# The low half of h in a split-fp32 feed-forward stage: GpSimdE's subtraction replaced by a ScalarE negation and an adding DMA

## The reference

```
x += 0.5 * (silu(rms(x) @ w1) * (rms(x) @ w3)) @ w2        # first feed-forward, d_ff = 2816
x += concat(window attention, gated chunk mixing) @ w_out + b_out
x += 0.5 * (silu(rms(x) @ w1') * (rms(x) @ w3')) @ w2'     # second feed-forward
x += sigmoid(rms(x) @ w_ple_gate) * (p @ w_ple_proj)
y  = rms(x)
```

## Time and profile before

| | |
|---|---|
| median of 3 runs | 987.37 us (985.55 to 987.81) |
| the profiled execution's own time | 986.51 us |
| its span, first to last instruction | 984.8 us |
| mean granted TensorE clock | 0.997 |
| TensorE matmul busy | 963.6 us, 98% |
| VectorE busy | 672.4 us, 68% |
| ScalarE busy | 458.7 us, 47% |
| GpSimdE busy | 260.5 us, 26% |
| h_lo on GpSimdE (L1101) | 18 instructions, 46.9 us |

### The profile page before, as it was taken

The page is one execution under the profiler, slowest core; times in us unless marked ns, Lnnn a source line. Parts: engine busy times, 40 slices in busy tenths (PEclk is TensorE's granted clock), DMA queues, the critical chain, the costliest instruction groups (busy, mean ns, idle before and its releaser), DMA issues.

```text
span 984.8 us, 19296 instructions
## 1 busy us (share of the span) xinstructions
PE 963.6 (98%) x7949; PEld 947.1 (96%) x7949; DVE 672.4 (68%) x1063; ACT 458.7 (47%) x750; POOL 260.5 (26%) x150
## 2 busy tenths in 40 slices
PE   6999999999999999999999999999999999999997
PEld 4999999999999999999899999999999999999997
DVE  5899658856768654457775399857766758855576
ACT  6645425533435443566444455424543443545243
POOL 2302202211111226332318411301221211114521
PEclk9999999999999999999999999999999999999999
DMA  7962433252243336321114693253324325235202
GB/s 216 163 127 70 124 105 99 76 145 72 75 128 99 97 85 184 102 65 44 44 55 129 128 172 97 61 145 97 96 80 116 97 60 144 65 98 161 87 22 88
DMA packets 191603, 101.38 MB, mean 103 GB/s; under 512 B 12955, under 2 KB 189429, under 8 KB 191501
## 3 DMA queue, kind: packets, MB, share of 16 engines
q1 hardware_dynamic: 175904, 90.23, 32.2%
q0 software_dynamic: 11440, 5.77, 4.7%
q10 hardware_dynamic: 4172, 4.15, 1.4%
HBM read 97.59 MB, written 3.59 MB: 103 GB/s over the span
## 4 chain that ended last, share of the span: by engine, by line
PE 91%; DVE 5%; ACT 1%; DMA 1%; issue 1%; SPq 0%; DVEq 0%; ACTq 0%
PE ps L1723 49%; PE ps L1803 36%; PE ps L2141 2%; PE ps L1759 1%; DMA x_rows<-in_x_prompt_dram 1%; PE ps L2015 1%; PE ps L2044 1%; DVE w_lo L1327 0%; PE ps L1754 0%; DVE w_lo L1419 0%; PE ps L1748 0%; DVE xb_lo L1216 0%; DVE tt L1437 0%; DVE mix_lo L1550 0%; PE ps L2165 0%
## 5 line engine op out<-in xcount | busy, mean ns | idle before, releaser
L1803 PE MATMUL ps<-xo_hi,w_hi 128*128 128x260 f32 x1008 | 284.2, 282 | 0.7 <-DVE ab L1350 0.7
L1803 PE MATMUL ps<-xo_lo,w_hi 128*128 128x260 f32 x1008 | 284.7, 282 | 0.0
L1803 PE MATMUL ps<-xo_hi,w_lo 128*128 128x260 f32 x1008 | 284.4, 282 | 0.0
L1723 PE MATMUL ps<-h_hi,w_hi 128*128 128x260 f32 x960 | 195.8, 285 | 0.7 <-issue 0.6
L1723 PE MATMUL ps<-h_hi,w_lo 128*128 128x260 f32 x960 | 193.4, 283 | 0.0
L1723 PE MATMUL ps<-h_lo,w_hi 128*128 128x260 f32 x960 | 193.4, 283 | 0.0
L1803 PEld LDWEIGHTS ps<-xo_hi,w_hi 128*128 128x128 f32 x1008 | 189.6, 188 | 0.9 <-issue 0.9
L1803 PEld LDWEIGHTS ps<-xo_hi,w_lo 128*128 128x128 f32 x1008 | 189.8, 188 | 0.0
L1803 PEld LDWEIGHTS ps<-xo_lo,w_hi 128*128 128x128 f32 x1008 | 189.7, 188 | 0.0
L1723 PEld LDWEIGHTS ps<-h_hi,w_hi 128*128 128x128 f32 x960 | 148.1, 189 | 1.7 <-issue 1.2
L1723 PEld LDWEIGHTS ps<-h_lo,w_hi 128*128 128x128 f32 x960 | 148.8, 189 | 0.0
(11 more groups left out here) (276 smaller groups left out, 1476.5 us busy)
## 6 DMA issues: line engine op xcount, KB each, us to landing
w_raw<-in_w_ffn_dram SPq DMA_DIRECT2D x88, 256.0 KB, 3.0
w_a<-in_w_ffn_dram SPq DMA_DIRECT2D x36, 512.0 KB, 4.8
w_raw<-in_w_ffn_dram SPq DMA_DIRECT2D x48, 384.0 KB, 3.2
w_raw<-in_w_ffn_dram SPq DMA_DIRECT2D x16, 512.0 KB, 7.0
w_lo<-in_w_ffn_dram POOLq DMA_DIRECT2D x11, 512.0 KB, 8.4
w_raw<-in_w_in_dram SPq DMA_DIRECT2D x10, 512.0 KB, 4.0
w_raw<-in_w_ple_gate_dram SPq DMA_DIRECT2D x8, 512.0 KB, 3.6
x_rows<-in_x_prompt_dram SPq DMA_DIRECT2D x4, 512.0 KB, 5.7
```

Of the source, the lines that this page charges most:

```text
L1723: ins = pe.matmul(ps[:, bank + step * h, 0:HALF], w[:, c, w0:w0 + P], m_[:, sk, h * HALF:(h + 1) * HALF], start=(first and n == 0), stop=( ...
L1803: ins = pe.matmul(ps[:, b, 0:Q], w[:, c, k * P:(k + 1) * P], m_[:, op, k, :], start=(first and k == 0 and n == 0), stop=(k == 3 and n == 2 ...
```

## The change

h_lo of the pairs 1 to 9 is made in two steps. ScalarE, right behind h_hi, writes -h_hi into h_lo; its wait is on its own h_hi. GpSimdE then issues a DMA from abuf to h_lo with accumulate, SBUF to SBUF, on one of two semaphores in turn. Down waits for the last two pairs of its chunk, the comb for pair p - 2 as before, now on the DMA's semaphore. VectorE's wait ahead of its subtraction of pair 10 is gone.

```diff
+        h_negated, h_added = sem("h_negated"), [sem(f"h_added{i}") for i in range(2)]
...
+        def h_lo_wait(eng, s, p):
+            if 0 < p < 10:
+                n = 9 * s + p - 1
+                eng.wait_ge(h_added[n % 2], 16 * (n // 2 + 1))
+            else:
+                eng.wait_ge(h_lo_ready, 2 * s + p // 10 + 1)
...  ScalarE, behind h_hi
+                        if 0 < p < 10:
+                            act.wait_ge(h_hi_ready, 11 * s + p + 1)
+                            nc.scalar.activation(flat(h_lo[:, k:k + 2, :]), flat(h_hi[:, k:k + 2, :]).bitcast(F32),
+                                                 ACT.Copy, scale=-1.0).then_inc(h_negated, 1)
...  GpSimdE
-                        pool.wait_ge(h_hi_ready, 11 * s + p + 1)
-                        nc.gpsimd.tensor_tensor(flat(h_lo[:, k:k + 2, :]), flat(abuf[:, p % 2, :, :]),
-                                                flat(h_hi[:, k:k + 2, :]).bitcast(F32),
-                                                ALU.subtract).then_inc(h_lo_ready, 1)
+                        n = 9 * s + p - 1
+                        pool.wait_ge(h_negated, n + 1)
+                        if n > 1:
+                            pool.wait_ge(h_added[n % 2], 16 * (n // 2))
+                        pool.dma_start(flat(h_lo[:, k:k + 2, :]), flat(abuf[:, p % 2, :, :]), accum_op=ALU.add
+                                       ).then_inc(h_added[n % 2], 16)
...  VectorE, comb of an even unit
-                                dve.wait_ge(h_lo_ready, 11 * s + p - 1)
+                                h_lo_wait(dve, s, p - 2)
...  VectorE, ahead of pair 0 and 10
-                        if p:
-                            dve.wait_ge(h_lo_ready, 11 * s + p)
...  TensorE, down
-                pe.wait_ge(h_lo_ready, 11 * s + pairs[n_pairs - 1] + 1)
+                for p in pairs[max(n_pairs - 2, 0):n_pairs]:
+                    h_lo_wait(pe, s, p)
```

## The result

The changed kernel takes 1041.55 us (median of 4 runs, 1039.53 to 1043.69), against 986.75 (985.55 to 987.81). The ratio is 1.0558, with a 95% interval of 1.0542 to 1.0573: 55 us slower. The profiled execution of the changed kernel spans 1041.4 us, 56.6 us more than before. At 1043.43 us it is 1.9 above the median of its kernel's four, so where two variants of the changed kernel lie a few microseconds apart, their traces and their medians can differ by as much.

What follows compares the result with a forecast made beforehand. TensorE was taken to bound the kernel, busy 963.6 of 984.8 us. Chunk stalls 35.2, comb 3.7, snap 0.2 and clock 15 sum to 54 us; on 986.5 that is 1040.6, forecast as 1041 us, range 1008 to 1072.

Steps and rivals of the forecast that it cites:

- Where h_lo is needed: At each of eight chunks, 2.66 to 3.26 us from h_hi's end to first use, and at unit 2's comb for pair 1.
- The landing time L: From the DMA's issue to its semaphore releasing the reader: 2.1 to first packet, 3.4 packets, 0.3 rest, 0.2 company; 6.0 us.
- The chunk stalls: TensorE's waits at eight chunks, each L + 1.26 minus the distance from h_hi's end to use: 8L - 12.8, 35.2 us.
- The fixed-plus-bandwidth rule: The skill page's 3.2 us landing would give chunk stalls of 12.8 us; without clock falls some +12, 999 us.
- Rival A: The DMA lands quickly, L from 3 to 5; at 4.0 about +31, 1018 us; chance 0.29.
- The comb of unit 2: VectorE's comb waits for pair 1, made in the same unit: stalls of 2.2 us in stage 0, 1.5 more in stage 1; 3.7.
- The snap: Product 6's snap, behind the negation on ScalarE, makes product 7 0.1 us late; hidden at chunks, shows for pair 4: 0.2 us.
- The clock: TensorE's clock halves after stalls: ten falls of 1.5 us each, 15 us; none would be 0, twice as long 30.
- Rival C: Not slower: without GpSimdE's subtraction VectorE's gate product of pair 1 no longer stretches, a hole closes, -1.0 us; chance 0.04.

Runs made afterwards that it cites:

- the copy: The changed kernel with its DMA as a plain copy of h over the negated high half, the addition left out: 1006.37 us, ratio 1.0186.
- The fill experiment: The changed kernel with 34 matmuls whose result is thrown away ahead of each chunk's wait for h_lo: 1030.50 us, ratio 1.0437.

## Why the prediction was right

The forecast was 1041 us, the measurement 1041.55. The mechanism is as put: eight chunk waits on the DMA, the comb of unit 2, the clock. That the number fits so closely is in part luck, since its terms were off in both directions: 35.2 + 3.7 + 0.2 + 15 in the forecast, and in the trace 32.7 + 4.9 + 0 + 18.3.

- *Where h_lo is needed.* This was right: at each chunk, and at the comb. The pairs with time to spare cost nothing (986.98 us with the DMA on four of them).
- *The landing time L.* I put it at 6.0. At the chunks the DMA landed 5.25 to 5.56 us after its issue, once 6.41, with 0.14 for the hand-over. The first packet came 1.4 us behind the issue at seven of the eight chunks, where I had 2.1 from the earlier trace rows. From the first packet to the end of the last it was 3.4 to 3.8 us at these seven, which my 3.4 + 0.2 meets, but not for my reasons: for pair 4, with its first packet as early, it was 2.9, and the DMA landed after 4.66 and 4.71 us. Why the packets are slower at the chunks was not tried.
- *The chunk stalls.* The term 8L - 12.8 = 35.2 runs from the end of h_hi to the chunk's first matmul, and on that stretch stand the DMA waits, 29.9, and the snap waits ahead of them, 2.8: 32.7 in all. With the measured landing (5.55 in the mean) L is 5.6 and the term 32. Its slope of eight holds: summed over the eight chunks the copy lands 16.4 us sooner (28.0 against 44.4), and its chunk waits are 16.4 less (13.5).
- *The fixed-plus-bandwidth rule.* The Trainium skill (page "DMA: Bandwidth & Descriptors", section "Anatomy of one DMA — SWDGE (gpsimd) path") gives a DMA from GpSimd 2.0 us and its bytes over 436 GB/s, here an estimate of 3.2 us. The plain copy does that in eight of its 18 DMAs (3.0 to 3.4 us, 3.21 at chunk 0), with a median of 4.2; the adding DMA does not, with 5.33 at chunk 0 and 4.7 at the least. Rival A, to which I gave 0.29, is the kernel with about the copy's landing time; I had put it at 1018 us, or 999 with the 3.2, and the kernel with the copy came out at 1006.
- *The comb of unit 2.* I put it at 3.7 and it measured 4.9; taking it out gave 5.0 with its share of the clock. L is larger there than at the chunks: in stage 0 the DMA was issued at 96.77 and the comb starts at 103.04, 6.3 us later, in stage 1 it was 6.6 (655.09 to 661.68). While its packets ran, other transfers moved 0.28 and 0.38 MB there, against 0.06 to 0.08 MB at seven of the eight chunks. Whether that is why it is larger was not tried.
- *The snap.* I put 0.2 for pair 4, and no snap wait stands there: 0. At the chunks I had it 0.1 us late and hidden under the stall. TensorE waits 0.2 to 0.9 us for it in five places, 2.8 in all. What I had wrong is the time from the end of h_hi to the start of product 7, which I took as unchanged. At chunk 1 it is 1.2 us in the kernel before (200.24 to 201.41), and in the changed kernel TensorE is there after 0.9 (209.97 to 210.90): h_hi itself comes later against TensorE. At chunk 3 the chain goes back from it over VectorE and ScalarE to a load of raw weights (353.21, 3.87 us). The wait is hidden all the same, as put: moving the negation away won nothing.
- *The clock.* I put ten falls of 1.5 us, 15. There were nine low stretches, five of 3.4 and four of 6.8 us, and they cost 18.3 us; pair 1 in stage 0 had none. My price was about right for a short stretch (1.64 us on the first tile of chunk 0, 1.70 at chunk 2); the long ones, behind the chunks 1 and 3, cost 2.2 to 2.8. The fill experiment shows the term by itself.
- *Rival C.* VectorE's relief came, 3.48 to 1.23 us, and was worth nothing beside a comb that waits for a DMA. Had by itself it is worth about 1.2 us.

## What to carry to other kernels

When the bounding engine takes over a result 0.25 us after it is ready, look at the time to completion of what replaces it, not at how busy the engines are: 2.4 us on a quarter-busy engine was free, and a DMA of 5.5 us in its place cost 55 us. Give a DMA only to results with more time to spare than its landing, or wait for it just ahead of the instruction that reads it. An idle time of some microseconds on TensorE is to be priced with the slow matmuls behind it, here half as much again.

## What the runs showed of the hardware

- In the changed kernel an adding DMA from SBUF to SBUF of 520 KB in rows of 4160 B took 4.7 us at the least and 5.8 in the median to land; as a plain copy 3.0 and 4.2 (18 of each). In pieces of 520 B, half of the bytes took 4.2 and 4.8.
- GpSimdE's issue of one took 0.57 us as a copy, 0.86 with 128 adding rows, 1.29 with 512 adding pieces.
- In all the traces here, from the first product of a feed-forward stage to its end, all 24 stalls of 3.8 us or more (from the start of one matmul to the start of the next) had half the clock at their end or behind them, and none of up to 2.0 us had. Between 2.1 and 3.5 us it came or it didn't: 2.9 us at pair 1 in stage 0 of the changed kernel had none, 3.2 us at the same place in stage 1 had one. Low stretches came in 3.4 or 6.8 us, and some began before TensorE had resumed.
- VectorE's product of 128x1040 took 1.23 us alone, and up to 3.48 with a subtraction of GpSimdE beside it.
